# Feed-forward's first product: the high and the low activations side by side in one matmul over 512 columns

## What is computed

```python
def swiglu(h, w_up, w_down):
    gate, up = jnp.split(h @ w_up, 2, axis=-1)
    return (jax.nn.silu(gate) * up) @ w_down
...
        h = rms_norm(x, g_pre_ffn[l]) * (1.0 + sc2) + sh2
        y = swiglu(h, w_up[l], w_down[l])
        x = x + g2 * rms_norm(y, g_post_ffn[l])
```

## Time and profile before

| | before |
|---|---|
| median of 3 runs | 490.85 us (490.51 to 491.58) |
| profiled execution, span | 489.1 us |
| what lies between the span and the median of the runs | 1.75 us |
| TensorE busy | 461.5 us, 94% of the span |
| VectorE busy | 299.8 us, 61% |
| ScalarE busy | 242.6 us, 50% |
| mean granted TensorE clock | 0.990 of full |

### The profile page before, as it was taken

One profiled execution on the slowest core, in us unless ns is written; L12 is line 12 of the kernel. 1 busy time (PEld: TensorE's weight loads), 2 busy tenths in 40 slices (PEclk: granted clock), 3 DMA queues, 4 the chain that ended last, 5 costly groups with the idle time before them and its releaser, 6 DMA issues.

```text
span 489.1 us, 8215 instructions
## 1 busy us (share of the span) xinstructions
PE 461.5 (94%) x3253; PEld 415.2 (85%) x3253; DVE 299.8 (61%) x487; ACT 242.6 (50%) x426; POOL 55.4 (11%) x96
## 2 busy tenths in 40 slices
PE   0859999999999999999999999999999999999994
PEld 0539888999899998898878789999999999999993
DVE  2056677768499968793679646673652563365215
ACT  5055545546576655656556337563553254345232
POOL 2000001100012130002578300000000000000000
PEclk9979999999999999999999999999999999999998
DMA  8998886586955673742645930799455645720002
GB/s 302 427 329 267 268 307 216 172 263 231 340 185 185 241 257 124 275 139 88 196 173 199 367 121 1 266 363 318 140 187 189 219 127 174 252 86 0 1 1 86
DMA packets 56370, 98.81 MB, mean 202 GB/s; under 512 B 5036, under 2 KB 41492, under 8 KB 53268
## 3 DMA queue, kind: packets, MB, share of 16 engines
q1 hardware_dynamic: 54036, 81.62, 48.7%
q0 software_dynamic: 2304, 16.78, 10.0%
HBM read 97.35 MB, written 1.05 MB: 201 GB/s over the span
## 4 chain that ended last, share of the span: by engine, by line
PE 89%; DMA 4%; DVE 2%; ACT 2%; SPq 1%; issue 1%; DVEq 0%; PEldq 0%; ACTq 0%
PE psum L1143 26%; PE psum L1144 25%; PE psum L1145 25%; DMA ada_end<-in_w_ada_dram 4%; PE psum L1401 3%; PE psum L1237 2%; PE psum L1236 1%; PE psum L1289 1%; PE psum L1354 1%; PE psum L1195 1%; PE psum L1263 1%; PE psum L1241 1%; PE psum L1271 1%; PE psum L1206 1%; DVE wlo L844 0%
## 5 line engine op out<-in xcount | busy, mean ns | idle before, releaser
L1143 PE MATMUL psum<-hhi,whi 128*128 128x256 f32 (+1 forms) x680 | 196.8, 289 | 3.9 <-DVE hlo L948 2.7
L1144 PE MATMUL psum<-hlo,whi 128*128 128x256 f32 (+1 forms) x680 | 192.7, 283 | 0.0
L1145 PE MATMUL psum<-hhi,wlo 128*128 128x256 f32 (+1 forms) x680 | 192.7, 283 | 0.0
L1143 PEld LDWEIGHTS psum<-hhi,whi 128*128 128x128 f32 (+1 forms) x680 | 130.0, 191 | 11.0 <-issue 4.2
L1144 PEld LDWEIGHTS psum<-hlo,whi 128*128 128x128 f32 (+1 forms) x680 | 130.3, 192 | 0.3
L1145 PEld LDWEIGHTS psum<-hhi,wlo 128*128 128x128 f32 (+1 forms) x680 | 130.1, 191 | 0.0
L844 DVE TENSOR_TENSOR wlo<-raw,whi 128x1024 fp32r<-128x1024 f32 (+4 forms) x92 | 92.5, 1035 | 22.1 <-ACT whi L588 21.7
L588 ACT ACTIVATE whi<-raw 128x1024 fp32r<-128x1024 f32 (+4 forms) x92 | 74.2, 841 | 18.3 <-DMA raw<-in_w_in_dram 16.3
L1094 DVE TENSOR_TENSOR dlo<-draw,dhi 128x2048 fp32r<-128x2048 f32 x11 | 25.1, 2293 | 57.1 <-ACT dhi L763 57.1
L1089 DVE TENSOR_TENSOR wlo<-raw,whi 128x1024 fp32r<-128x1024 f32 x40 | 47.0, 1219 | 2.7 <-ACT whi L756 2.7
L763 ACT ACTIVATE dhi<-draw 128x2048 fp32r<-128x2048 f32 x11 | 20.9, 1911 | 43.9 <-PE psum L1145 43.9
(11 more groups left out here) (160 smaller groups left out, 605.0 us busy)
## 6 DMA issues: line engine op xcount, KB each, us to landing
raw<-in_w_up_dram SPq DMA_DIRECT2D x22, 1024.0 KB, 7.6
xn<-in_w_ada_dram POOLq DMA_DIRECT2D x16, 1024.0 KB, 5.2
raw<-in_w_in_dram SPq DMA_DIRECT2D x7, 2048.0 KB, 9.2
draw<-in_w_down_dram SPq DMA_DIRECT2D x11, 1024.0 KB, 5.3
raw<-in_w_in_dram SPq DMA_DIRECT2D x4, 1280.0 KB, 7.1
raw<-in_w_in_dram SPq DMA_DIRECT2D x3, 1536.0 KB, 6.7
raw<-in_w_ada_dram SPq DMA_DIRECT2D x2, 2048.0 KB, 9.7
ada_end<-in_w_ada_dram SPq DMA_DIRECT2D x4, 1024.0 KB, 16.9
```

Of the source, the lines that this page charges most:

```text
L1143: pe.matmul(dst, a[0], b[0], start=first, stop=False)
L1144: pe.matmul(dst, a[0], b[1], start=False, stop=False)
L1145: return pe.matmul(dst, a[1], b[0], start=False, stop=last)
```

## The change

hhi and hlo become the two halves of one tensor `hcut` [128, 8, 2, 256], so that for each k the high and the low activations lie side by side, 512 columns in a row. In steps 1 to 10 the first product then has two matmuls for each (j, a, k) in place of three: the high weights against all 512 columns, and the low weights against the high activations, added onto the second half (columns 256 to 511). The first half of the bank then holds high by high, the second half the two other terms. A bank thus holds one (j, a), and each step writes four banks, B_UP. VectorE adds the two halves with a tensor_reduce over pairs of columns a distance of 256 apart: `gate_sum` into fsil, from where silu now reads, and the up sum into the new buffer usum, from where the product reads. The counts on up_done are doubled, since each (j, a) now counts. TensorE waits for the sums of the step before (gate_summed, u_summed), before it rewrites a bank, in place of f_ready of two steps before. Step 0 keeps its product, its banks and its reads from PSUM (`whole`), and the second half of up(1) waits for its f.

```diff
--- before.py
+++ after.py
@@ -235,8 +235,8 @@
         whi = [sb(f"whi{i}", [P, KC * BANK], F32R) for i in range(2)]
         wlo = [sb(f"wlo{i}", [P, KC * BANK], F32R) for i in range(2)]
         xt = sb("xt", [P, TT, D])
-        hhi = sb("hhi", [P, KC, S], F32R)
-        hlo = sb("hlo", [P, KC, S], F32R)
+        hcut = sb("hcut", [P, KC, 2, S], F32R)
+        hhi, hlo = hcut[:, :, 0, :], hcut[:, :, 1, :]
         xn = sb("xn", [P, TT, D])
         hx = xn[:, :, :].rearrange("p t (k n) -> p t k n", n=P)
         ada_part = xn[:, :, :].rearrange("p t n -> p (t n)")
@@ -294,6 +294,7 @@
         dhi = [sb(f"dhi{i}", [P, 2, D], F32R, scope=ffn) for i in range(2)]
         dlo = [sb(f"dlo{i}", [P, 2, D], F32R, scope=ffn) for i in range(2)]
         fsil = [sb(f"fsil{i}", [P, 2, S], scope=ffn) for i in range(2)]
+        usum = sb("usum", [P, 2, S], scope=ffn)
         fhi = [sb(f"fhi{i}", [P, 2, S], F32R, scope=ffn) for i in range(2)]
         flo = [sb(f"flo{i}", [P, 2, S], F32R, scope=ffn) for i in range(2)]
         ffn.close()
@@ -304,6 +305,7 @@
         B_ROWS = (7, B_ADA, B_T)
         B_Y = ((6, 0), (4, 6))
         B_TURNED = (2, 4)
+        B_UP = ((2, 3), (0, 1))
 
         ada_in = [sem(f"ada_in{k}") for k in range(KC // 2, KC)]
         part_in = sem("part_in")
@@ -338,6 +340,7 @@
         up_done, down_done, silu_done, f_ready, f_hi, f_lo = (sem("up_done"), sem("down_done"), sem("silu_done"),
                                                              sem("f_ready"), sem("f_hi"), sem("f_lo"))
         d_hi, d_lo, up_hi, up_lo = sem("d_hi"), sem("d_lo"), sem("up_hi"), sem("up_lo")
+        gate_summed, u_summed = sem("gate_summed"), sem("u_summed")
 
         block = ctx.enter_context(nc.Block())
 
@@ -446,7 +449,7 @@
                     sp.wait_ge(w_hi, 4 * (B_WO + 1 + i))
                     sp.wait_ge(w_lo, 4 * (B_WO + 1 + i))
                 elif third:
-                    sp.wait_ge(up_done, 2)
+                    sp.wait_ge(up_done, 4)
                 else:
 
                     sp.wait_ge(up_hi, 4 * (i - 2))
@@ -752,7 +755,7 @@
                     if first:
                         act.wait_ge(units, BLOCK_DONE[B_WO + 1])
                     else:
-                        act.wait_ge(up_done, 2 * (i - 1))
+                        act.wait_ge(up_done, 4 * (i - 1))
                 act.activation(block_view(whi[slot], B_FFN)[:, 2 * q:2 * q + 2, :],
                                block_view(raw[slot], B_FFN)[:, 2 * q:2 * q + 2, :], ACT.Copy).then_inc(up_hi, 1)
 
@@ -790,10 +793,15 @@
             for t in range(TT):
                 cut_h(t)
 
-            def silu_tile(i, slot, j):
-
-                act.wait_ge(up_done, 2 * i + j + 1)
-                act.activation(fsil[slot][:, j, :], bank[2 * (1 - slot) + j][:, 0:S], ACT.Silu).then_inc(silu_done, 1)
+            def silu_tile(i, slot, j, whole):
+
+                if whole:
+                    act.wait_ge(up_done, 2 * (j + 1))
+                    src = bank[j][:, 0:S]
+                else:
+                    act.wait_ge(gate_summed, 2 * (i - 1) + j + 1)
+                    src = fsil[slot][:, j, :]
+                act.activation(fsil[slot][:, j, :], src, ACT.Silu).then_inc(silu_done, 1)
 
             def f_part(i, slot, j):
                 act.wait_ge(f_ready, 2 * i + j + 1)
@@ -803,12 +811,12 @@
                 if not last:
                     for q in range(4 if first else 2):
                         cut_up_hi(i + 1, 1 - slot, q, first)
-                silu_tile(i, slot, 0)
+                silu_tile(i, slot, 0, first)
                 if not last and not first:
                     for q in range(2, 4):
                         cut_up_hi(i + 1, 1 - slot, q, first)
                 f_part(i, slot, 0)
-                silu_tile(i, slot, 1)
+                silu_tile(i, slot, 1, first)
                 if first:
                     cut_down_hi(0, 1, True)
                 if not last:
@@ -1101,10 +1109,28 @@
             for t in range(TT):
                 cut_h(t)
 
-            def f_tile(i, slot, j):
-
+            def halves_sum(dst, src):
+
+                return dve.tensor_reduce(dst, src.rearrange("p (a s) -> p s a", a=2), AX_X, ALU.add)
+
+            def gate_sum(i, slot, j):
+
+                if j == 0:
+                    dve.wait_ge(f_hi, 2 * (i - 1))
+                dve.wait_ge(up_done, 4 * i + 2 * j + 1)
+                halves_sum(fsil[slot][:, j, :], bank[B_UP[j][0]]).then_inc(gate_summed, 1)
+
+            def f_tile(i, slot, j, whole=False):
+
+                if whole:
+                    dve.wait_ge(silu_done, j + 1)
+                    dve.tensor_tensor(fsil[slot][:, j, :], bank[j][:, S:2 * S], fsil[slot][:, j, :], ALU.mult).then_inc(f_ready, 1)
+                    return
+                dve.wait_ge(up_done, 4 * i + 2 * j + 2)
+                halves_sum(usum[:, j, :], bank[B_UP[j][1]]).then_inc(u_summed, 1)
                 dve.wait_ge(silu_done, 2 * i + j + 1)
-                dve.tensor_tensor(fsil[slot][:, j, :], bank[2 * (1 - slot) + j][:, S:2 * S], fsil[slot][:, j, :], ALU.mult).then_inc(f_ready, 1)
+                dve.wait_ge(u_summed, 2 * (i - 1) + j + 1)
+                dve.tensor_tensor(fsil[slot][:, j, :], usum[:, j, :], fsil[slot][:, j, :], ALU.mult).then_inc(f_ready, 1)
 
             def f_rest(i, slot, j):
                 dve.wait_ge(f_hi, 2 * i + j + 1)
@@ -1114,12 +1140,16 @@
                 if not last:
                     for q in range(4 if first else 2):
                         cut_up_lo(i + 1, 1 - slot, q)
-                f_tile(i, slot, 0)
+                if not first:
+                    gate_sum(i, slot, 0)
+                f_tile(i, slot, 0, first)
                 if not last and not first:
                     for q in range(2, 4):
                         cut_up_lo(i + 1, 1 - slot, q)
                 f_rest(i, slot, 0)
-                f_tile(i, slot, 1)
+                if not first:
+                    gate_sum(i, slot, 1)
+                f_tile(i, slot, 1, first)
                 if first:
                     cut_down_lo(0, 1)
                 if not last:
@@ -1409,7 +1439,7 @@
                 first_up(0, j)
             turn_x(1, 1)
             for j in range(2):
-                first_up(1, j).then_inc(up_done, 1)
+                first_up(1, j).then_inc(up_done, 2)
 
             def up(i, slot, first):
 
@@ -1417,21 +1447,26 @@
                     pe.wait_ge(up_hi, 4 * i)
                     pe.wait_ge(up_lo, 4 * i)
                 for j in range(2):
-                    if first:
+                    if first and j == 0:
                         pe.wait_ge(h_lo, 8)
-                    else:
-
-                        pe.wait_ge(f_ready, 2 * (i - 2) + j + 1)
-                    dst = bank[2 * (1 - slot) + j]
+                    if first and j == 1:
+                        pe.wait_ge(f_ready, 2)
                     for a in range(2):
+                        if not first:
+                            if a == 0:
+                                pe.wait_ge(gate_summed, 2 * (i - 2) + j + 1)
+                            else:
+                                pe.wait_ge(u_summed, 2 * (i - 2) + j + 1)
+                        dst = bank[B_UP[j][a]]
                         for k in range(KC):
                             if first and j == 0 and a == 0 and k % 2 == 0:
 
                                 pe.wait_ge(up_hi, k // 2 + 1)
                                 pe.wait_ge(up_lo, k // 2 + 1)
-                            w = [block_view(x[slot], B_FFN)[:, k, FSTEP * a + P * j:FSTEP * a + P * (j + 1)] for x in (whi, wlo)]
-                            mm = three(dst[:, S * a:S * (a + 1)], w, [hhi[:, k, :], hlo[:, k, :]], k == 0, k == KC - 1)
-                    mm.then_inc(up_done, 1)
+                            wh, wl = [block_view(x[slot], B_FFN)[:, k, FSTEP * a + P * j:FSTEP * a + P * (j + 1)] for x in (whi, wlo)]
+                            pe.matmul(dst[:, :], wh, hcut[:, k, :, :].rearrange("p a s -> p (a s)"), start=k == 0, stop=False)
+                            mm = pe.matmul(dst[:, S:2 * S], wl, hhi[:, k, :], start=False, stop=k == KC - 1)
+                        mm.then_inc(up_done, 1)
 
             def down_part(i, slot, t, n, first, last):
                 for j in range(2):
```

## The result

The changed kernel takes 487.62 us (median of 4 runs, 486.76 to 487.85) beside 490.68 us for the kernel before (4 runs, 490.40 to 491.58). The ratio is 0.9924 with a 95% interval of 0.9910 to 0.9937: faster by 3.1 us between the medians, and by 3.7 us (3.1 to 4.4, ratio times 490.68) as the ratio has it.

The account below looks back on a forecast made before the run. TensorE was taken to set the pace, by the distance between matmul starts. Saved matmul time of 3.84 us less one wait of 1.0 us gave -2.8 us, so 488.0 us; range 487.0 to 490.4 us.

Parts of the forecast that it names:

- the columns' line: TensorE matmuls of 256, 384 and 512 columns: each costs some 0.0135 us beyond its columns, at every width.
- The matmul term: First products of steps 1 to 10: joining matmuls saves 0.38 us a step, 3.84 us in ten steps.
- gap rule: Warm TensorE matmuls: columns at 2.4 GHz plus 2.5 ns each, so 320 matmuls fewer would save only 0.8 us.
- The reductions: VectorE's four sums per step, 0.69 us each, cost nothing in settled steps while each stays below some 3.4 us.
- It waits 1.0 us, once.: TensorE at the start of step 2 waits 1.0 us for step 1's last low quarter of w_up.
- rival 4: The wait in step 1 doesn't show, because the block comes earlier or silu is served sooner: 487.0 us; chance 0.07.
- The range: Whole kernel: 487.0 to 490.4 us, from no wait to most of the way to nothing saved.
- the faster columns: Joined matmuls in the first products at 0.2260 us each, as late in a down product: saving 4.5 us.
- Rival 1: Alternating widths in the first products keep 0.2311 us per 512-column matmul: saving 2.85, wait 0.9, 488.9 us; chance 0.2.
- A product of pairs as dear as three matmuls: First products: a 512-column matmul behind a 256 costs 0.24 us, nothing is saved, 491.5 us; chance 0.13.
- slow reductions: VectorE's sums slow on strided pairs: at 2.3 us each the gain is gone, at 2.9 us 492.0 us; chance 0.05.

Follow-up runs that it names:

- split version: The changed kernel with each joined 512-column matmul made two of 256 again, all else kept: 491.72 us, ratio 1.0015 to the kernel before.
- late changed kernel: The changed kernel with the load of block 2 of w_up also waiting for f of step 0: 492.07 us, ratio 1.0013 to the kernel before.

## Why the prediction was partly right

- **The bound, and the columns' line.** Right. TensorE has no gap in a settled step before or after, and a pair takes 0.347 us.
- **The matmul term, "ten steps 3.84 us".** Right in mechanism, and 3.70 us in size from up(1) to the last matmul. Eight settled steps and step 2 save some 0.4 us each in the product where 0.38 was forecast; product 1 saves 0.20 (11.59 to 11.39), and a down product behind a settled joined one takes 5.49 us in place of 5.47. The pair was forecast at 0.228 + 0.120 = 0.348 us and takes 0.347. Its parts came out otherwise: between starts the joined matmul has 0.232 us and the short one behind it 0.115, so the sum came out right with two terms some 0.004 us off, one each way, which is luck. Undoing the join alone took all of it away.
- **The Trainium skill's gap rule** ("TensorE: Matmul & The Clock Gate", "Back-to-back issue gap"), 0.8 us by the prediction's estimate for 320 matmuls. The page calls it the gap of an isolated matmul. The runs don't agree with it, neither here (3.70 us) nor where the down products were split (3.1 us in the trace for 264).
- **The reductions.** Right: 0.68 us each against R = 0.69, hidden in settled steps, and hidden there still when made twice (a wait of 0.6 us came in step 1 alone).
- **"It waits 1.0 us, once."** This step failed: the sum had -3.84 + 1.0 = -2.8 us, and the trace has -3.70 and a wait of nothing. The longer chain was right (324.96 - 317.14 = 7.82 us from arrival, measured 7.85), and in the split version, where the block comes as late as before, the wait is 1.0 to 1.1 us. What failed is that I took the block's arrival in the trace of before as a fixed time, because its load is triggered by step 0. It came 1.1 to 1.5 us earlier against up(1) in all six profiles with joined matmuls and no added wait, and in the changed kernel the chain then fits, with 0.3 us or less to spare. In rival 4 I even named the early block and gave it 0.07, since "both orders are fixed by the program". An order is fixed by the program, a landing isn't.
- **The range.** It ended at 487.0 us, at the case with no wait. That case was what happened, so the measured time lies on its very edge (0.04 us below by the ratio). My own sum without the wait is 487.0; the edge should have left room below it for the 4.5 us of the faster columns, which makes 486.4.
- **The rivals.** Rival 1's slow distance of 0.2311 us is what the joined matmuls do show (0.232 in a settled step), but its loss didn't come, as the short matmul behind each is as much quicker. A product of pairs as dear as three matmuls (0.36) and slow reductions didn't occur. Rival 4, with a chance of 0.07, is the one that came true, by the early block.

What stays open is why the block comes earlier. Block 2 is loaded in two halves. The DMA view of the issue of the second one alone (window 307.98 to 308.10 before, 307.57 to 307.70 changed) gives the us from issue to landing, before and changed:

```profile
raw<-in_w_up_dram SPq DMA_DIRECT2D x1, 1024.0 KB, 9.0
```

```profile
raw<-in_w_up_dram SPq DMA_DIRECT2D x1, 1024.0 KB, 7.9
```

In all eleven profiles of the table it is issued 0.69 us behind up(1), and the transfers of both forms run at the same rates, 340 to 410 GB/s. A load ends with sixteen completions, which the traces' semaphore records show. Fifteen of the sixteen are in at 8.34 to 8.52 us in all eleven; only the last one differs, 8.46 to 8.59 us with joined matmuls and 9.72 to 9.96 us with those of 256 columns. So the block is early or late by one completion. The load behind it (w_down's) lands at 12.36 to 12.57 us in all eleven, its last completion 0.5 to 1.6 us behind the fifteenth. A straggling completion is thus there with either form; with joined matmuls only block 2's is spared. A packet of instructions (16 KB, 1.1 us long) runs beside the end of block 2's load. It starts 7.70 to 7.87 us behind up(1) in the six profiles with the early block and 7.19 to 7.69 us in the five with the late one. With the block delayed on purpose fifteen completions are in at 10.2 us, the packet starts ahead of that in all three kernels (7.17, 8.51 and 8.75 us), and the last completion comes at 11.7 us in all three. A packet that holds up the one DMA engine that fetches it, and block 2 where it comes in time to do so, fits all fourteen profiles. It is still only argued: the border between 7.69 and 7.70 us is narrow, the records don't name the engine, and no run moved the packet alone.

## What to carry to other kernels

Two matmuls of 256 columns with the same stationary operand, whose moving operands can lie side by side, were worth joining where TensorE sets the pace: here each one less gave 0.0116 us (3.70 us over 320), with the extra work hidden on an engine that has half of each step free. Ask for the one place where that engine isn't free, here the first step behind a late transfer, and price the chain from the transfer's landing on. But take the landing as a range, since a change of TensorE's instructions moved it here by 1.1 to 1.5 us.

## What the runs showed of the hardware

- The distance from a 512-column start to the next isn't one number. In the second half of a down product it is 0.226 us, in a joined product 0.232 us, with 0.115 for the 256-column matmul between two of them (0.120 among its like). A joined pair takes 0.347 us; in one product of some profiles all pairs behind the first take 0.353 us, and the product 11.39 us. That was product 1 in four of the eight profiles with joined matmuls, product 2 in the changed kernel's second profile, and the rest of product 2 behind the lower clock in the late changed kernel; two profiles have none. Where product 1 didn't have it, it took 11.18 us, with a first pair of 0.43. What sets it wasn't looked into.
- A distance of 3.5 us between two matmul starts was followed by the lower clock and cost 1.8 us on top of itself; those of 1.3 and 2.2 us were not. This makes the price of a wait jump: 1.1 us longer in idling went with 2.75 us between the medians of two kernels (492.07 and 489.32).
- A transfer issued at the same place landed 1.1 to 1.5 us earlier beside fewer, larger matmuls, and by one of its sixteen completions alone. With its issue 1.85 us later the difference was gone (11.8 us in all three kernels).
